# A two-layer decoder step on one core: sample tile and second halves of the out projection in another order, and other homes for early expert weights

## The reference, cut to what matters

```python
y = jnp.concatenate([a_out, b_out], -1) @ w_out                  # 1024 -> 1024: the out projection
xp = _layernorm(ALPHA * xp + yp, ln_g[layer, 0], ln_b[layer, 0])
...
scores = jax.nn.sigmoid(h.astype(F32) @ w_router.astype(F32))    # 16 experts in 4 groups
...                                                              # best group, its top 2, normalised gates
for e in range(N_EXPERTS):
    he = jax.nn.silu(h @ w_gate[e]) * (h @ w_up[e])
    y = y + gates[:, e:e + 1] * (he @ w_down[e])
...
xp = _layernorm(ALPHA * xp + _moe(xp, ...), ln_g[layer, 1], ln_b[layer, 1])
```

## Time and profile before

| | |
|---|---|
| median of 3 runs | 1132.19 us (1129.57 to 1136.82) |
| the profiled execution: its time, its span | 1131.82 us, 1130.0 us |
| TensorE busy, share of the span | 1015.4 us, 90% |
| VectorE, ScalarE, GpSimd busy | 514.4, 377.1, 201.8 us |
| HBM read, written | 206.28 MB, 46.89 MB |
| TensorE's clock over the span | 0.945 of full speed |

### The profile page before, as it was taken

How to read it: one execution, slowest core, us unless ns; L and a number is a source line. 1 busy time by engine, 2 the same in 40 slices (tenths; PEclk the granted TensorE clock), 3 DMA queues, 4 the chain that set the end, 5 groups by cost and what they waited for, 6 DMA issues and landing times.

```text
span 1130.0 us, 25899 instructions
## 1 busy us (share of the span) xinstructions
PE 1015.4 (90%) x10322; PEld 675.5 (60%) x10322; DVE 514.4 (46%) x1303; ACT 377.1 (33%) x943; POOL 201.8 (18%) x236
## 2 busy tenths in 40 slices
PE   8999996799979399999989999999999967999792
PEld 3687454566645157777788887655555535666450
DVE  1581135323443503579644555776542343235344
ACT  0102114145544322423234333154541241455442
POOL 0010000214543200000021011321000002146431
PEclk9999998699999699999989999899999986999996
DMA  9754205899998343122322224286553157999961
GB/s 317 293 88 158 98 38 215 277 372 354 360 346 281 114 146 112 38 90 78 87 77 76 69 77 137 80 327 215 197 198 150 56 207 275 380 356 358 353 227 39
DMA packets 82720, 218.02 MB, mean 193 GB/s; under 512 B 13598, under 2 KB 54606, under 8 KB 64240
## 3 DMA queue, kind: packets, MB, share of 16 engines
q1 hardware_dynamic: 65184, 155.38, 39.0%
q0 software_dynamic: 17408, 60.89, 16.2%
HBM read 206.28 MB, written 46.89 MB: 224 GB/s over the span
## 4 chain that ended last, share of the span: by engine, by line
PE 68%; DMA 11%; DVE 9%; issue 5%; POOL 4%; ACT 2%; POOLq 0%; DVEq 0%; SPq 0%; ACTq 0%
PE bank L1324 10%; PE bank L1594 9%; PE bank L1419 7%; DMA work<-parts,final_row 7%; PE bank L1502 6%; PE bank L1693 4%; PE bank L1528 3%; PE bank L1443 3%; PE bank L1565 2%; DMA acc<-parts,final_row 2%; DMA out_x_dram<-acc,final_row 2%; PE bank L1947 1%; PE bank L1972 1%; PE bank L1335 1%; PE bank L1349 1%
## 5 line engine op out<-in xcount | busy, mean ns | idle before, releaser
L1324 PE MATMUL bank<-ring,cat 128*128 128x512 f32 x256 | 112.6, 594 | 1.3 <-ACT cat L2125 1.3
L1594 PE MATMUL bank<-xT,ring 128*128 128x288 f32 x448 | 110.9, 407 | 0.0
L1594 PEld LDWEIGHTS bank<-xT,ring 128*128 128x128 f32 x448 | 84.6, 190 | 23.8 <-issue 1.1
L1419 PE MATMUL bank<-ring,work 128*32 128x128 f32 (+1 forms) x1344 | 84.1, 320 | 1.7 <-DVE work L2522 1.7
L1324 PEld LDWEIGHTS bank<-ring,cat 128*128 128x128 f32 x256 | 47.5, 190 | 57.2 <-issue 57.2
L1419 PEld LDWEIGHTS bank<-ring,work 128*32 128x32 f32 (+1 forms) x1344 | 58.6, 123 | 26.1 <-issue 14.5
L1502 PE MATMUL bank<-xT,ring 128*128 128x288 f32 x256 | 63.1, 407 | 0.0
L1502 PEld LDWEIGHTS bank<-xT,ring 128*128 128x128 f32 x256 | 48.3, 190 | 13.5 <-issue 0.4
L2535 DVE SCALAR_TENSOR_TENSOR work<-work,stat 96x1024 f32<-96x1024 f32 x22 | 28.2, 1281 | 49.1 <-DMA work<-parts,final_row 26.7
L2103 ACT COPY work<-bank 32x256 f32<-32x256 f32 x120 | 43.5, 363 | 13.8 <-PE bank L1443 12.5
L2365 DVE SCALAR_TENSOR_TENSOR acc<-x,bank 128x512 f32<-128x512 f32 x16 | 11.0, 687 | 76.4 <-PE bank L1324 76.4
(11 more groups left out here) (473 smaller groups left out, 2063.3 us busy)
## 6 DMA issues: line engine op xcount, KB each, us to landing
ring<-in_stream_dram SPq DMA_DIRECT2D x61, 1024.0 KB, 9.7
work<-in_stream_dram SPq DMA_DIRECT2D x16, 1024.0 KB
cat<-in_stream_dram SPq DMA_DIRECT2D x16, 1024.0 KB
by_batch<-in_pages_dram SPq DMA_DIRECT2D x128, 128.0 KB, 2.4
x<-in_stream_dram SPq DMA_DIRECT2D x12, 1024.0 KB, 19.2
xT<-in_stream_dram SPq DMA_DIRECT2D x12, 1024.0 KB, 17.8
lnp<-in_ln_dram POOLq DMA_DIRECT2D x4, 1024.0 KB
xkept<-x POOLq DMA_DIRECT2D x8, 512.0 KB, 2.9
```

Source lines behind the costliest of these rows:

```text
L1324: i = pe.matmul(bank(n)[0:ROWS[tile], :], cat[:, k, tok(tile)], slot(w[k // 4], 4, 512)[:, k % 4, :], start=(k == 0), stop=(k == KC - 1))
L1419: i = pe.matmul(by_half[rows * q:rows * q + rows, :, to:to + width], xgT[:, e % 2, k, at:at + rows], w[:, :, width * q:width * q + width], ...
L1594: i = pe.matmul(bank(n + s)[:, 0:nn], slot(w, KC, 256)[:, k, P * (m % 2):P * (m % 2) + P], xT[:, k, a:a + nn], start=(k == 0), stop=(k == ...
```

## The change

1. TensorE's order. Layer 0: all first halves and the sample tile, then the second halves, each followed by what it lets go: o0 o1 o2 o3 o4 p0 mT4 p1 rt4 mT0 p2 rt0 mT1 p3 rt1 mT2 rt2 mT3 rt3. Layer 1: mT0 o2 rt0 mT1 o3 rt1 o4 p2 mT4 p3 rt4 mT2 rt2 mT3 rt3. Tile 3 is the last to be normed instead of the sample tile. VectorE, ScalarE and POOL's `xkept` follow the order of the norms (`NORMED`).
2. The transposed tiles go to `cat` instead of `xT`, and the router reads them there.
3. The homes `xT` and `cat` change places in `SPARE`. `xT` is now filled together with `work`, before the out projection; `cat` behind `x`, after T1.
4. The first two blocks of the out projection are given free at o4, the other two at p3.
5. The tiles whose logits VectorE copies are 4, 0, 1 in layer 0 and 0, 1 in layer 1.

```diff
-FRONT = [("o", 0), ("p", 0), ("o", 1), ("mT", 0), ("p", 1), ("rt", 0), ("o", 2), ("mT", 1), ("p", 2), ("rt", 1),
...
+FRONT = [("o", 0), ("o", 1), ("o", 2), ("o", 3), ("o", 4), ("p", 0), ("mT", 4), ("p", 1), ("rt", 4), ("mT", 0),
...
+NORMED = [[tile for kind, tile in front if kind == "mT"] for front in FRONTS]
-COPIED = 3
+COPIED = [(4, 0, 1), (0, 1)]
...
-SPARE = [("work", 0), ("work", 1), ("cat", 0), ("cat", 1), ("x", 0), ("x", 1), ("xT", 0), ("xT", 1)]
+SPARE = [("work", 0), ("work", 1), ("xT", 0), ("xT", 1), ("x", 0), ("x", 1), ("cat", 0), ("cat", 1)]
...
-AHEAD = [NSLOT + i for i, (home, _) in enumerate(SPARE) if home != "xT"]
+AHEAD = [NSLOT + i for i, (home, _) in enumerate(SPARE) if home != "cat"]
...
-        block(("wout", layer, n), job(f"{layer}.o{NT - 1}"))
+        block(("wout", layer, n), job(f"{layer}.o{NT - 1}") if n < 2 else job(f"{layer}.p{LAST}"))
...
-                    for j in AHEAD[0:2]:
+                    for j in AHEAD[0:4]:
                         load_spare(key[1], j)
...
-                    take(sp, job(f"{layer}.o{NT - 1}"))
-                    for j in AHEAD[2:4]:
-                        load_spare(layer, j)
...
             def mixture(layer):
                 L = f"{layer}."
-                for tile in range(NT):
+                for tile in NORMED[layer]:
                     if (layer, tile) != (1, 0):
                         spread(2 * layer, tile)
-                    if tile == NT - 1:
-                        router_scores(layer, 0)
-                        router_scores(layer, 3)
-                    copy_xT(f"{L}mT{tile}", tile)
-                router_scores(layer, 4)
+                    if tile == LAST:
+                        copied_scores(layer)
+                        for other in NORMED[layer][:-1]:
+                            if other not in COPIED[layer]:
+                                router_scores(layer, other)
+                    copy_xT(f"{L}mT{tile}", tile, cat)
+                router_scores(layer, LAST)
...
+                if layer == 0:
+                    for tile in range(LAST + 1):
+                        add_output(layer, 0, tile)
+                    norm_output(layer, 4)
+                    norm_output(layer, 0)
+                    copy_logits(layer, 4)
+                    norm_output(layer, 1)
+                    copy_logits(layer, 0)
+                    norm_output(layer, 2)
+                    copy_logits(layer, 1)
+                else:
+                    norm_output(layer, 1)
+                    add_output(layer, 0, 2)
+                    copy_logits(layer, 0)
+                    add_output(layer, 0, 3)
+                    copy_logits(layer, 1)
+                    norm_output(layer, 4)
+                    norm_output(layer, 2)
+                norm_output(layer, LAST)
```

More of the change, by code:

```diff
@@ L672, in landed_all, with nth @@
             landed(eng, *JOBS[name])
+        def nth(k, tile):
+            return NT * k + (NORMED[k // 2].index(tile) if k % 2 == 0 else tile) + 1
         def rows_in(e):
@@ L1310, in turn_x @@
                 for g in range(2):
-                    pe.wait_ge(ln_done if g else ln_left, NT * norm + tile + 1)
+                    pe.wait_ge(ln_done if g else ln_left, nth(norm, tile))
                     n = job(name, g)
@@ L1343, in router_logits @@
                     n = job(f"{L}rt{tile}")
-                    if tile == 0:
+                    if tile == NORMED[layer][0]:
                         pe.wait_ge(router_loaded, 32)
@@ L1348, in router_logits @@
                     for k in range(KC):
-                        i = pe.matmul(bank(n)[0:ROWS[tile], 0:N_EXP], xT[:, k, tok(tile)], wr[:, k, :],
+                        i = pe.matmul(bank(n)[0:ROWS[tile], 0:N_EXP], cat[:, k, tok(tile)], wr[:, k, :],
                                       start=(k == 0), stop=(k == KC - 1))
@@ L2010, in copy_xT @@
                     take(act, n)
-                    give(act.copy(xT[:, 4 * g:4 * g + 4, tok(tile)], bank(n, 4, P)[:, :, 0:ROWS[tile]]), n)
+                    give(act.copy(to[:, 4 * g:4 * g + 4, tok(tile)], bank(n, 4, P)[:, :, 0:ROWS[tile]]), n)
             def spread(k, tile):
                 r = ROWS[tile]
-                act.wait_ge(ln_var, NT * k + tile + 1)
+                act.wait_ge(ln_var, nth(k, tile))
                 act.activation(squares[k % 2][0:r, :], acc[0:r, tile, :], ACT.Square, bias=mv[0:r, tile, 0:1], scale=-1.0,
@@ L2017, in spread, with copied_scores @@
                                accum_out=mv[0:r, tile, 1:2]).then_inc(ln_spread, 1)
-                act.wait_ge(ln_spread, NT * k + tile + 1)
+                act.wait_ge(ln_spread, nth(k, tile))
                 act.activation(rstd[0:r, tile:tile + 1], mv[0:r, tile, 1:2], ACT.Sqrt, bias=c("lneps", r),
                                scale=1.0 / D_MODEL).then_inc(ln_std, 1)
-            def router_scores(layer, tile):
[L2023 to L2030, removed]
+            def copied_scores(layer):
+                act.wait_ge(logits_ready, layer + 1)
+                if NT - 1 in COPIED[layer]:
+                    act.activation(score[0:NS, NT - 1, :], logit[0:NS, NT - 1, :], ACT.Sigmoid)
+                act.activation(score[:, 0:2, :], logit[:, 0:2, :], ACT.Sigmoid).then_inc(scores_ready, 1)
@@ L2032, in mixture @@
+            def router_scores(layer, tile):
+                r = ROWS[tile]
+                n = job(f"{layer}.rt{tile}")
+                take(act, n)
+                give(act.activation(score[0:r, tile, :], bank(n)[0:r, 0:N_EXP], ACT.Sigmoid), n)
             def mixture(layer):
                 L = f"{layer}."
-                for tile in range(NT):
+                for tile in NORMED[layer]:
                     if (layer, tile) != (1, 0):
                         spread(2 * layer, tile)
-                    if tile == NT - 1:
-                        router_scores(layer, 0)
-                        router_scores(layer, 3)
-                    copy_xT(f"{L}mT{tile}", tile)
@@ L2386, in norm_output @@
                 else:
-                    for half in range(2):
-                        if layer == 0 or ("op"[half], tile) not in EARLY:
-                            add_output(layer, half, tile)
+                    if layer == 0 or ("p", tile) not in EARLY:
+                        add_output(layer, 1, tile)
                     for half in range(2):
@@ L2411, in copy_logits @@
                 take(dve, n)
-                give(dve.tensor_copy(logit[:, tile, :], bank(n)[:, 0:N_EXP]), n)
-                if tile + 1 == COPIED:
+                r = ROWS[tile]
+                give(dve.tensor_copy(logit[0:r, tile, :], bank(n)[0:r, 0:N_EXP]), n)
+                if tile == COPIED[layer][-1]:
                     landed(dve, n, 1)
@@ L2419, in route @@
                 dve.wait_ge(router_loaded, 32)
-                for tile in range(COPIED, NT):
-                    landed(dve, job(f"{layer}.rt{tile}"), 1)
+                for tile in range(NT):
+                    if tile not in COPIED[layer]:
+                        landed(dve, job(f"{layer}.rt{tile}"), 1)
                 step(dve.tensor_tensor(biased, score, rbias.unsqueeze(1).broadcast_to([P, NT, N_EXP]), ALU.add))
```

27 lines of the change are left out of this document (10 added, 17 removed).

## The result

The changed kernel took 1136.39 us (median of 18 runs, 1132.26 to 1138.84) against 1132.38 us for the kernel before (18 runs): ratio 1.0029, 95% interval 1.0016 to 1.0042. It is slower by about 3.3 us by this ratio; the two medians lie 4.0 us apart. I had forecast 1131.5 us, no change. The time lies inside the range and far within 1%, but that is luck as far as the mechanism goes: the range reached to 1137 for the sake of the norm parameters, which cost nothing, and none of my rivals had the cause.

The account below looks back on a forecast made before the run. TensorE was taken to bound the out projection and transfers the expert stage, so T1 counted. From the profiled 1131.82 us, gains of 0.1 (layer 0) and 0.2 (layer 1) gave 1131.5 us, range 1126.5 to 1137.

Parts of the forecast that it names:

- T1: Moment in each layer when expert 0's rows have been transposed; forecast 0.1 us earlier in layer 0, 0.2 in layer 1.
- the norm parameters: Layer 1's parameter load, end of attention: SP's 4 MB instead of 2 MB beside it would not delay it, cost 0.
- The bytes before T1, the homes: Fills issued before T1: nine blocks before and after, xT's fills swapped with cat's, costed at nothing.
- the rival with 0.12: Layer 1: SP's 4 MB make the norm parameters land late, full price 4.4 us, 1135.9 us; chance 0.12.
- The last product 2.12 us earlier: Out projection, layer 0: with less work ahead of it, p3 ends at 180.58 instead of o4 at 182.70.
- Both holds, square only 0.43 us earlier: After p3, VectorE's logits copy (layer 0) and ScalarE's mT2 copies (both layers) delay tile 3's square; 0.43 us gain remains.
- The tail on 128 rows, "+0.3 for all": From the last tile's square on: 128 rows instead of 64 cost 0.3 us in layer 0, between 0 and 1.0.
- My 0.1 for the router: Last router, layer 0, on 128 rows instead of 64: 0.1 us longer if nothing overlaps.
- The sum: Whole kernel: 1131.82 us less 0.1 for layer 0 and 0.2 for layer 1 gives 1131.5 us.
- The expert stage moves whole with T1: Expert stage, either layer: bound by transfers, it keeps its length and shifts as a whole with T1.

Follow-up runs that it names:

- Edit 4: Changed kernel with tile 2's transposes directly behind p3 and tile 1's layer 0 logits no longer copied by VectorE; 0.9996 of the kernel before.
- edit 3: Changed kernel with one unneeded 512-column matmul in each of TensorE's three waits of the tail; 0.9991 of the kernel before.
- experiments 7 to 10: Unneeded matmuls in routing waits: kernel before (tail too), 0.9968; changed kernel, transposes first (tail too), 0.9971; fewer, routing only: Edit 4, 0.9968; kernel before, 0.9969.
- experiments 4 and 5: The first is Edit 4, 0.9996; the second adds to it one unneeded 512-column matmul ahead of mT3 and one ahead of rt3, 1.0002 of the kernel before.

## Why the prediction was wrong

- *The bytes before T1, the homes.* Right: nine blocks on either side, and the homes alone give 0.9996.
- *The norm parameters, cost 0.* Right, by the same even shares of the two queues; the rival with 0.12 fell.
- *The last product 2.12 us earlier.* Right in layer 0: 2.19 us (67.90 against 70.09 from the first product); in layer 1 it was 1.63 (75.37 against 77.00). The fit is partly luck: I took the router of the sample tile at 1.69 us and it took 1.04 from start to start, while its transposes took 0.64 instead of 0.44 and two of the halves 7.07 instead of 6.87.
- *Both holds, square only 0.43 us earlier.* Right in kind: 0.73 and 0.72 us earlier. ScalarE's square began 3.17 us after p3's end, I had 3.41. Edit 4 moved it another 1.74 us.
- *The tail on 128 rows, "+0.3 for all", "if none of it overlaps ... 1.0".* This is the step that failed. From the square to the end of the last router it measured +2.87 us in layer 0 (1.08 + 1.79) and +2.07 in layer 1 (0.37 + 1.70). I took the durations of 128-row transposes and routers from places ahead of the last product, where the clock is full, and set them where it isn't. At full clock (edit 3, layer 0) the same tail costs 0.46 + 0.16 = 0.6 us more than before, inside my bounds; the rest is the clock. My 0.1 for the router was the largest miss: twice the columns at the half clock cost 1.79 and 1.70 us, where at the full clock they cost 0.83 (1.93 - 1.10). The evidence stood in the earlier trace rows: 1.78 us for a router on 64 rows and 1.69 for one on 128 cannot both be at full clock. The 64-row router that ran at full clock in the changed kernel took 1.10:

```profile
160.23 1.10 PE L1351 MATMUL bank<-router,cat 128*64 128x16 f32 x16
```

- *The sum.* 1131.82 - 0.3 should have been 1131.82 - 1.45 (two squares) + 4.94 (two tails) - 0.09 = 1135.2, the last term being the routing; from the median of the 18 runs before, 1132.38, it is 1135.8, against 1136.39 measured. The terms are measured ones, so this shows only that nothing else is missing, not that the rows of before gave them.
- *The expert stage moves whole with T1.* Good enough for this change (3.4 us at T1, 3.3 in the time), but the four kernels with additions in the routing show that it isn't so in general. That expert 0's own speed counts as well is my reading; it was not tested by itself.

A router's matmul has 16 moving columns, and its weights are the token columns: 128 for a prompt tile, 64 for the sample tile. Loading them takes nearly all of its time, 3.49 of 3.56 us in the changed kernel and 1.69 of 1.77 before (layer 0; the first line is after, the second before):

```profile
187.22 3.49 PEld L1351 LDWEIGHTS bank<-router,cat 128*128 128x128 f32 x16 [1.09 <-ACT cat L2013]
188.68 1.69 PEld L1349 LDWEIGHTS bank<-router,xT 128*64 128x64 f32 x16 [0.62 <-issue]
```

At the same clock twice the columns take nearly twice as long, 1.93 against 1.10 us at full clock and 3.56 against 1.86 at half. The Trainium skill (TensorE: Matmul & The Clock Gate, section LDWEIGHTS) says that a weight load's time goes by its columns and not by its rows. On the columns the trace agrees; on the rows no run here shows it. So moving the sample tile from the last place doubled the weight columns of the one router that nobody can hide.

Open: whether the clock's fall, 3.2 to 6.4 us after the last product where nothing was added, depends on anything in the order but chance, and what carries the gain of experiments 7 to 10, which have the same time at very different T1.

## What to carry to other kernels

Price an operation at the clock of the place it moves to, not of the place it comes from: when TensorE's last large products are done and a serial tail of small matmuls follows, look at the granted clock of that tail, and keep in it the tile with the fewest weight columns. Here an order that finished the last big product 2.19 us earlier lost, since it left more small work behind it, on TensorE and on the in-order engines. And where TensorE waits some us on the path, a few unneeded matmuls can be worth their time, but only as many as end before the wait does. At the half clock such a matmul took twice as long here (2.05 against 1.02 us), and then it became the wait itself.

## What the runs showed of the hardware that I had not expected

- TensorE's clock halved while the engine was hardly idle. Between the last product's end (178.7) and the fall (184.3) it stood still for 0.77 us and for the last 0.3; all the rest was routers of 16 columns and transposes. In experiments 4 and 5 there was no idle gap at all in that place (busy for 1.00 of each us, from 180 to 186 and from 178 to 184), and the clock fell all the same, 5.1 and 4.0 us after the last product. With one 512-column matmul in each of the changed kernel's three waits (experiment 3) it stayed at 1.00 until 190.4; the row of 183 to 191:

```profile
183.00:191.00 8.00, 6.38 (x44) 5.01 (x44) 3.52 (x11) 5.59 (x12) 0.53 (x1) 0.96 0.55 227
```

- Adding work to an idle engine on the critical path made the whole program 0.3% faster (experiments 7 to 10), with 12 or 10 unneeded matmuls a layer in the routing. How the gain reaches the end of the program is open, as said above.
